# Small work moved, a halved load, a finer last pair and another order of the routing in a one-layer decoder kernel

## The reference

```python
h = rmsnorm(x, g_mix)
pa, pb, pc, pd = split(h @ w_in)            # w_in: 1024 x 2816
o_a = moba_attention(...)                   # four branches, 4 heads of 64 each
o_b = diff_attention(..., lam, ...)         # lam = exp(lq1.lk1) - exp(lq2.lk2) + 0.2
o_c = stick_breaking_attention(...)
o_d = sliding_window_attention(...)         # A, B, D add a relative position bias (table of 32 buckets)
merged = sum(sigmoid(h @ w_gate[i]) * (branches[i] @ w_br[i]) for i in range(4))
x = x + merged @ w_o                        # w_o: 1024 x 1024
x = x + hierarchical_moe(rmsnorm(x, g_ffn), ...)  # top group of 4, top 2 of its 8 experts
out = rmsnorm(x, g_final)
```

## Time and profile before

| | |
|---|---|
| device time, median of 3 runs (lowest to highest) | 717.75 us (717.66 to 717.78) |
| the profiled execution, its own time | 719.13 us |
| its span | 717.3 us |
| TensorE busy | 685.7 us, 96% |
| VectorE busy | 245.9 us, 34% |
| ScalarE busy | 192.0 us, 27% |
| GpSimd busy | 4.2 us, 1% |
| moved by DMA | 243.56 MB, mean 340 GB/s |

### The profile page before, as it was taken

How to read it: one execution, slowest core, us unless ns; L and a number is a source line. 1 busy time by engine, 2 the same in 40 slices (tenths; PEclk the granted TensorE clock), 3 DMA queues, 4 the chain that set the end, 5 groups by cost and what they waited for, 6 DMA issues and landing times.

```text
span 717.3 us, 9888 instructions
## 1 busy us (share of the span) xinstructions
PE 685.7 (96%) x4042; PEld 401.6 (56%) x4042; DVE 245.9 (34%) x526; ACT 192.0 (27%) x304; POOL 4.2 (1%) x8
## 2 busy tenths in 40 slices
PE   8999999999999999999999999999989899898995
PEld 6899887777777874344344344344334343442432
DVE  7463556766567673121121121122121020210212
ACT  5551565598563521100100100001000010000112
POOL 0000000000000000000000000000000000000000
PEclk9999999999999999999999999999999999998998
DMA  8899631374439978999999999999999999999992
GB/s 308 284 273 286 215 117 59 118 259 152 176 118 343 406 307 292 409 428 426 426 427 426 425 428 426 429 426 428 428 429 426 429 427 428 424 428 429 414 399 104
DMA packets 46125, 243.56 MB, mean 340 GB/s; under 512 B 10192, under 2 KB 13448, under 8 KB 33800
## 3 DMA queue, kind: packets, MB, share of 16 engines
q1 hardware_dynamic: 45640, 241.45, 84.6%
q0 software_dynamic: 448, 1.59, 0.7%
HBM read 241.96 MB, written 1.07 MB: 339 GB/s over the span
## 4 chain that ended last, share of the span: by engine, by line
PE 63%; DMA 22%; SPq 6%; DVE 5%; ACT 2%; issue 2%; POOLq 0%; DVEq 0%; ACTq 0%
PE bank L1713 21%; DMA unit<-in_w 20%; PE bank L1768 8%; PE bank L1386 7%; PE bank L1387 7%; PE bank L1388 7%; SPq L548 5%; PE bank L1691 4%; DMA unit<-in_w_in 2%; DVE low L332 2%; PE bank L1780 1%; PE bank L1781 1%; PE bank L1742 1%; PE bank L1478 1%; ACT high L327 1%
## 5 line engine op out<-in xcount | busy, mean ns | idle before, releaser
L1713 PE MATMUL bank<-unit,xT 128*64 128x512 f32 x1024 | 230.8, 604 | 14.0 <-DMA unit<-in_w 12.3
L1713 PEld LDWEIGHTS bank<-unit,xT 128*64 128x64 f32 x1024 | 76.0, 139 | 153.5 <-issue 147.1
L1768 PE MATMUL bank<-unit,hidT 128*64 128x512 f32 x480 | 106.3, 595 | 0.0
L1386 PE MATMUL bank<-high,hT_hi 128*128 128x512 f32 (+2 forms) x208 | 79.8, 384 | 2.4 <-DVE low L332 2.4
L1387 PE MATMUL bank<-low,hT_hi 128*128 128x512 f32 (+2 forms) x208 | 77.3, 372 | 0.0
L332 DVE TENSOR_TENSOR low<-unit,high 128x2048 fp32r<-128x2048 f32 (+1 forms) x34 | 70.7, 2099 | 11.4 <-ACT high L327 11.4
L1768 PEld LDWEIGHTS bank<-unit,hidT 128*64 128x64 f32 x480 | 33.1, 137 | 61.5 <-issue 60.0
L1388 PE MATMUL bank<-high,hT_lo 128*128 128x512 f32 (+2 forms) x176 | 65.1, 370 | 0.0
L327 ACT ACTIVATE high<-unit 128x2048 fp32r<-128x2048 f32 (+1 forms) x34 | 58.9, 1756 | 8.4 <-PE bank L1388 5.1
L1263 DVE TENSOR_TENSOR y_lo<-bank,y_hi 128x512 fp32r<-128x512 f32 x30 | 20.7, 691 | 94.1 <-ACT y_hi L793 94.1
L1691 PEld LDWEIGHTS bank<-pick,hk 128*128 128x128 bf16 x768 | 44.4, 98 | 13.5 <-issue 12.2
(11 more groups left out here) (252 smaller groups left out, 688.0 us busy)
## 6 DMA issues: line engine op xcount, KB each, us to landing
unit<-in_w SPq DMA_DIRECT2D x86, 2048.0 KB, 30.1
unit<-in_w_gate SPq DMA_DIRECT2D x8, 2048.0 KB, 9.9
unit<-in_w SPq DMA_DIRECT2D x12, 1024.0 KB, 26.6
unit<-in_w SPq DMA_DIRECT2D x14, 512.0 KB, 9.0
unit<-in_w_in SPq DMA_DIRECT2D x3, 2048.0 KB, 15.9
unit<-in_w_br SPq DMA_DIRECT2D x4, 1024.0 KB, 6.0
unit<-in_w_o SPq DMA_DIRECT2D x2, 2048.0 KB, 10.6
unit<-in_w_in SPq DMA_DIRECT2D x6, 512.0 KB, 7.6
```

The costliest lines, as they stand in the source:

```text
L1386: mm(dst, a_hi, b_hi, start=first, stop=False)
L1713: last = mm(bank[4 + w][g * CAP:(g + 1) * CAP, :], xT[:, k, g * CAP:(g + 1) * CAP], rhs, start=(k == 0), stop=(k == KD - 1))
L1768: last = mm(bank[6 + n][g * CAP:(g + 1) * CAP, :], hidT[:, c, g * CAP:(g + 1) * CAP], rhs[:, c, n * BANK:(n + 1) * BANK], start=(c == 0), ...
```

## The change

Nine edits, all in the order or grain of work; the arithmetic stays but for one subtraction.

1. Stage 1, loads: unit 1 comes in two loads of 1 MB with a semaphore each, and ScalarE's first high part of it waits for the first half alone.
2. Stage 1, small work: on VectorE `dvec` moves behind the copy of block 5, the other small operations behind the low parts of unit 4, the end of lam behind those of unit 5; the exponential on ScalarE moves behind the high parts of unit 5. 23 instead of 18 idle products at the very start.
3. Start of stage 2: of the three waits for banks read out, the one for bank 4 moves behind the first scores.
4. Step 7: a low part goes ahead of the sums of squares.
5. Stage 3: half of `branch(3, 3)` goes ahead of the first `turn_tile`.
6. Routing: x is turned by blocks of 128 neighbouring columns (`turn_rows`) with router weights loaded to match and a second copy of g_ffn (1024 elements of 4 bytes); three quarters of the turning stand ahead of the end of the last w_o product, and router products and absorptions behind it. 36 idle products for 20. `remain(3)` goes to GpSimd; on ScalarE the squares and norm of the last quarter go ahead of its first part. The slot numbers are raised by one once, so that the subtraction at line 1199 goes.
7. The last pair: 12 pieces for 9; `combine(p - 1, [0])` goes ahead of `up(1)`; hidden, its turning, and its copy go in two halves, the second in bank 5.
8. Stores: in the order in which the parts are ready.
9. The overflow branch, which is not run here, waits for matrices in pairs.

The core of the diff:

```diff
-LAST_PIECES = ((0, 0, 0, 0, 4), (0, 0, 0, 4, 8), (0, 2, 0, 0, 4), (0, 2, 0, 4, 6), (0, 2, 0, 6, 8),
-               (0, 4, 0, 0, 4), (0, 4, 1, 0, 2), (0, 4, 1, 2, 3), (0, 4, 1, 3, 4))
+LAST_PIECES = ((0, 0, 0, 0, 4), (0, 0, 0, 4, 8),
+               (0, 2, 0, 0, 2), (0, 2, 0, 2, 4), (0, 2, 0, 4, 6), (0, 2, 0, 6, 7), (0, 2, 0, 7, 8),
+               (0, 4, 0, 0, 2), (0, 4, 0, 2, 4), (0, 4, 1, 0, 2), (0, 4, 1, 2, 3), (0, 4, 1, 3, 4))
...
+                if u == 1:
+                    sp.dma_start(dst[:, 0:4, :], src[:, 0:4, :]).then_inc(s["second_half"], 16)
+                    dst, src = dst[:, 4:, :], src[:, 4:, :]
                 sp.dma_start(dst, src).then_inc(s_unit[u % RING1], 16)
...
-            for t in range(NT):
-                for n in range(2):
-                    sp.wait_ge(*((s[("half0", "half1")[t]], 1) if n == 0 else (s["scaled"], t + 1)))
-                    cols = slice(n * BANK, (n + 1) * BANK)
-                    sp.dma_start(out[0, t * P:(t + 1) * P, cols], xg[:, t, cols]).then_inc(s["stored"], 16)
+            for t, n, ready, count in ((0, 1, s["scaled"], 1), (1, 0, s["half1"], 1), (1, 1, s["scaled"], 2), (0, 0, s["half0"], 1)):
+                sp.wait_ge(ready, count)
+                cols = slice(n * BANK, (n + 1) * BANK)
+                sp.dma_start(out[0, t * P:(t + 1) * P, cols], xg[:, t, cols]).then_inc(s["stored"], 16)
...
+            t, cols, qs = quarter(3)
+            pool.wait_ge(s["parts1"], 4)
+            pool.wait_ge(s["parts3"], 2)
+            nc.gpsimd.tensor_tensor(remainder[1][:], x[:, t, cols].rearrange("p (q k) -> p k q", k=KD), hk_1[:, t, :, qs],
+                                    ALU.subtract).then_inc(s["remains"], 1)
...
-            act.wait_ge(s["lamx"], 1)
-            nc.scalar.activation(lam[:, 2:4], lam[:, 0:2], ACT.Exp).then_inc(s["lame"], 1)
             for u in range(6):
...
                 for half in range(2 if u < 5 else 0):
                     high_part(act, u + 2, half)
+                if u == 3:
+                    act.wait_ge(s["lamx"], 1)
+                    nc.scalar.activation(lam[:, 2:4], lam[:, 0:2], ACT.Exp).then_inc(s["lame"], 1)
...
                         nc.vector.tensor_scalar(dst, src, scale, None, ALU.mult).then_inc(s["projD"], 1)
+                    if i == 5:
+                        bias_vectors()
                 for half in range(2 if u < 5 else 0):
                     low_part(dve, nc.vector, u + 2, half)
+                if u == 2:
+                    constants()
+                elif u == 3:
+                    weight_of_difference()
...
+            branch(3, 3, [0])
             pe.wait_ge(s["mrg"], 14)
-            turn_tile(0, merged, s["mTps"])
-            branch(3, 3)
+            turn_tile(0)
+            branch(3, 3, [1])
...
+            for b in (0, 1):
+                read_out(b)
             scores_ahead(0)
+            read_out(4)
...
             first_part(2)
             second_part(2)
-            first_part(3)
             row_squares(3)
             second_norm(1)
+            first_part(3)
             second_part(3)
...
             weighted_turned(1, 1)
-            remain(3)
             second_norm(1)
...
-            link(V.tensor_scalar(slot[:], slot[:], -1.0, None, ALU.add))
...
+                for half, done in enumerate((s["last_half"], z["hid"])):
+
+                    of = lambda ap: ap.rearrange("p (q c) -> p q c", c=CE)[:, :, 2 * half:2 * half + 2]
+                    V.scalar_tensor_tensor(out=of(hid[:]), in0=of(sg[:]), scalar=slot_gate[:], in1=of(bank[5][:]),
+                                           op0=ALU.mult, op1=ALU.mult).then_inc(done, 1)
...
+                    combine(main, p - 1, [0])
                     up(1, main, p, slots, here)
-                    combine(main, p - 1, [0])
-                    turn_hidden(main, p)
+                    turn_half(main, p, 0)
                     combine(main, p - 1, [1])
+                    turn_half(main, p, 1)
```

More of the change, by code:

```diff
@@ L185, in hybrid_decoder_layer @@
         wo_lo = place("wo_lo", [P, KD, TOK], F32R, offset=shared)
+        h2T = [place(f"h2T{t}", [P, KD, TOK], offset=(hT_at, shared)[t]) for t in range(NT)]
         sig_at = at[0]
@@ L318, in high_part @@
                 act.wait_ge(first_pieces[piece], 16)
+            elif xi == 1 and piece == 0:
+                act.wait_ge(s["second_half"], 16)
             else:
@@ L782, in experts @@
                     link(nc.scalar.activation(warm, warm, ACT.Sqrt))
-                act.wait_ge(z["hTp"], p + 1)
                 if not first:
                     act.wait_ge(z["Y"], 2 * p)
-                nc.scalar.activation(hidT[:].rearrange("p c q -> p (c q)"), bank[4][:], ACT.Copy).then_inc(z["hT"], 1)
+                if last:
+                    for half, (ready, done) in enumerate(((s["last_half"], s["last_half"]), (z["hTp"], z["hT"]))):
+                        act.wait_ge(ready, 2 if half == 0 else p + 1)
+                        nc.scalar.activation(hidT[:, 2 * half:2 * half + 2, :].rearrange("p c q -> p (c q)"),
+                                             bank[4 + half][:, 0:TOK], ACT.Copy).then_inc(done, 1)
+                else:
+                    act.wait_ge(z["hTp"], p + 1)
+                    nc.scalar.activation(hidT[:].rearrange("p c q -> p (c q)"), bank[4][:], ACT.Copy).then_inc(z["hT"], 1)
                 if not first:
@@ L1132, in second_norm, with logits @@
                 V.reciprocal(rs[:, t:t + 1], rs[:, t:t + 1]).then_inc(s["rs"], 1)
+            def logits(t):
+                dve.wait_ge(s["lg_ps"], t + 1)
+                dve.wait_ge(s["rs"], t + 1)
+                return V.scalar_tensor_tensor(out=lg[:, t, :], in0=bank[4 + t][:, 0:NG + NE], scalar=rs[:, t:t + 1],
+                                              in1=rbias[:], op0=ALU.mult, op1=ALU.add)
             add_product(0, 0).then_inc(s["x1"], 1)
@@ L1160, in _ @@
             from_end = lambda n: cst[:, C_IOTA:C_IOTA + n].unsqueeze(1).broadcast_to([P, NT, n])
-            R = NG + NE
-            for t in range(NT):
-                dve.wait_ge(s["lg_ps"], t + 1)
-                dve.wait_ge(s["rs"], t + 1)
-                link(V.scalar_tensor_tensor(out=lg[:, t, :], in0=bank[4 + t][:, 0:R], scalar=rs[:, t:t + 1],
-                                            in1=rbias[:], op0=ALU.mult, op1=ALU.add))
             link(V.tensor_reduce(m[:, 0, :], lg[:, :, 0:NG], AX, ALU.max))
@@ L1245, in gathered, with hidden @@
                                     ALU.mult).then_inc(z["xT"], 1)
-            def hidden(z, p, first=False):
+            def hidden(z, p, first=False, last=False):
                 dve.wait_ge(z["sg"], p + 1)
@@ L1270, in experts @@
                     picks(main, p + 1, p + 1)
-                hidden(main, p, first)
+                hidden(main, p, first, last)
                 if not last:
@@ L1608, in _, with turn_tile, turn_rows @@
             branch(D_, 1, [0])
-            def turn_tile(t, rows, done):
+            def turn_tile(t):
                 for i in range(2):
                     for kk in range(4):
-                        k_th = rows[:, t, :].rearrange("p (q k) -> p k q", k=KD)[:, 4 * i + kk, :]
+                        k_th = merged[:, t, :].rearrange("p (q k) -> p k q", k=KD)[:, 4 * i + kk, :]
                         last = nc.tensor.transpose(bank[2 * t + i][:, kk * P:(kk + 1) * P], k_th, ident)
-                    last.then_inc(done, 1)
+                    last.then_inc(s["mTps"], 1)
+            def turn_rows(t, i):
+                pe.wait_ge(s["x1"], TURNED[t, i])
+                for k in range(4 * i, 4 * i + 4):
+                    last = nc.tensor.transpose(bank[2 * t + i][:, (k % 4) * P:(k % 4 + 1) * P], x[:, t, k * P:(k + 1) * P], ident)
+                last.then_inc(s["h2ps"], 1)
             def out_product(t, n, ks=range(KD)):
@@ L1724, in turn_hidden, with turn_half @@
                 last.then_inc(z["hTp"], 1)
+            def turn_half(z, p, half):
+                pe.wait_ge(*((z["hid"], p + 1) if half else (s["last_half"], 1)))
+                for c in range(2):
+                    c_th = hid[:].rearrange("p (q c) -> p c q", c=CE)[:, 2 * half + c, :]
+                    last = nc.tensor.transpose(bank[4 + half][:, c * P:(c + 1) * P], c_th, ident)
+                last.then_inc(z["hTp"] if half else s["last_half"], 1)
             def turn_picks(z, p):
```

114 lines of the change are left out of this document (63 added, 51 removed).

## The result

The changed kernel takes 720.34 us (median of 20 runs, 718.22 to 726.15) against 717.82 for the kernel before (20 runs, 717.42 to 720.18): a ratio of 1.0037, 95% interval 1.0026 to 1.0048, so 2.5 us slower. The forecast was 720.7. The profiled execution has a span of 719.3 us against 717.3. The stream of expert weights is full to the end as before and starts later.

The account below looks back on a forecast made before the run. It took the DMA stream of expert weights as the bound, shifted by TensorE's first up product; +2.9 + 2.3 - 0.7 + 0 - 0.3 - 0.45 - 0.8 = +2.95 us on the 717.75 median gave 720.7, range 716.6 to 723.4.

Parts of the forecast that it names:

- the wait released by `dvec`: Sign in stage 1: TensorE idle about 5 us before block 7, until VectorE's dvec, directly behind unit 2's low parts.
- the half clock behind it: Sign in stage 1: a granted clock of 0.5 in the windows from 38 to 41 us.
- the missing idle rows before unit 1's halves: Sign in stage 1: TensorE no longer has idle rows before the two halves of unit 1.
- Stage 1, +5.2 less 0.7: Up to the scores: waiting for dvec +2.9 us, clock loss +2.3; moved wait for bank 4 at the scores -0.7.
- Step 7, 0: Low part ahead of the sums of squares: ScalarE's root still runs at 151.4, so 0 us (-0.3 to +0.3).
- branch(3, 3) in halves, -0.3: Stage 3: TensorE's 0.80 us idle before 227.69 is filled; out_product starts at 229.8 instead of 230.06, -0.3 us.
- Routing, -0.45: Before the experts: new order of turnings and router products 0.2 us earlier, slot subtraction gone -0.25; -0.45 (-1.0 to +0.2).
- The term for the subtraction: Routing: the subtraction of slots, 0.19 us at 264.62, goes with the gap behind it, -0.25 us.
- GpSimd's subtraction: Routing rival: remain(3) on GpSimd blocks VectorE's chain over the shared SBUF interface, 1.6 to 3.2 us more; chance 0.10.
- The end, -0.8: Last pair and stores: finer pieces and new order -0.3 us, stores issued as ready -0.5; -0.8 (-2.4 to 0).
- A fixed time after the first up product: Expert stage: the weight stream ends a fixed time after that product, so each microsecond there is one of the whole.
- unit 2 early, and all edits earn: Stage 1 rival: unit 2 lands at 26 instead of 30.2, no clock fall, -3.55 us, 714.2; chance 0.15.

Follow-up runs that it names:

- e6: The kernel before with only VectorE's small work and lam's exponential moved as in the change, dvec behind unit 2's low parts: 720.42 us, ratio 1.0034.
- e1: The changed kernel with dvec made ahead of unit 2's low parts: 713.52 us, ratio 0.9941 to the kernel before.
- e4: The changed kernel with 18 idle products on TensorE in the wait for dvec: 720.91 us, ratio 1.0044 to the kernel before.
- e2: The changed kernel with step 7 as before, sums of squares ahead of the low part: 718.38 us, ratio 1.0013 to the kernel before.
- e8: e3 with remain(3) taken back from GpSimd to VectorE: 713.35 us, ratio 0.9938 to the kernel before.
- e3: The changed kernel with dvec ahead of unit 2's low parts and step 7 as before: 713.47 us, ratio 0.9937 to the kernel before.
- e9: e3 with the four stores issued in the order of before: 715.57 us, ratio 0.9968 to the kernel before.
- e5: The kernel before with only unit 1 loaded in two halves: 716.60 us, ratio 0.9980.
- e10: e3 with the last pair as before (nine pieces, hidden rows in one product, combine behind up): 714.11 us, ratio 0.9951 to the kernel before.
- e7: The kernel before with only the small work and lam's exponential moved, but dvec ahead of unit 2's low parts: 716.74 us, ratio 0.9983.

## Why the prediction was right, and where it was not

Direction, size and the deciding mechanism were right: `dvec` behind the low parts makes TensorE wait at block 7, the clock falls behind it, and the later start of the experts carries it to the end. e6 shows that the moved small work alone makes the loss, and e1 that putting `dvec` back ahead of the low parts turns the whole change into a gain of 4.3 us. But the sum was right by luck, because two terms were wrong in opposite ways: up to the first up product it had +3.75 and the traces show +3.73, of which the scores have 2.25 instead of 4.5 and step 7 has 1.9 instead of 0. On the profiled executions the whole sum, +2.95, was too large: their spans differ by 2.0. Of the signs named ahead, the wait released by `dvec`, the half clock behind it and the missing idle rows before unit 1's halves are there; the low parts of unit 2 started at 31.00, a little ahead of the forecast 32.

- **Stage 1, +5.2 less 0.7: mis-sized.** Measured +2.25 at the scores. Unit 2 landed at 29.05, not 30.2, so block 7 started at 36.33 instead of 37.6 and waited 4.42 instead of 5.4: its load was issued 0.5 earlier than before and took 15.2 us instead of 15.9. The clock missed 1.71 us of full speed and cost 1.3 at the scores, by e4, not 2.3. These two, 1.3 and 1.0, are the 2.25 by which the term was too large. In the traces of e2 and e6 the landing is at 30.30 and 30.09, the clock misses 3.41 us of full speed, and the scores are 4.25 and 5.04 late (e6 has the 0.56 ahead of the scores still): the 4.5 of the forecast is inside what single executions show. I took the spread of one load for a constant.
- **Step 7, 0: the step that failed.** The prediction said that the root could not run before 151.4 "the same", because it added the low part's 2.28 and the sums' 1.4 to 147.7. It left out that the low part must wait for ScalarE's high part: here 0.45 us before 150.48, with the stage 2.25 late. The root came 2.70 late, not 2.25, and TensorE lost as much to the chain behind it as it gained by the vanished 0.78, and 0.4 more. Against the changed kernel e2 measured 2.0 us; the waits are 0.4 of that, the rest appears with a fall of the clock that two other traces of the same order don't have.
- **branch(3, 3) in halves, -0.3:** -0.2 measured (4.15 to 3.95).
- **Routing, -0.45:** -0.22. The term for the subtraction held (-0.25 against -0.23), that for the order did not: behind the last w_o product it takes 4.2 us instead of 4.7 as forecast 4.1, but that product now ends 0.5 later by the turnings inside it (258.69 against 254.23, from a start 3.95 late), and the two cancel.
- **GpSimd's subtraction.** Rows: it ran from 261.77 to 263.17, and VectorE's logits at 263.00 and its chain at 263.29 and 263.48 kept their pace, 0.16 and 0.17 an instruction. e8 finds no difference in time. The rule of the Trainium skill ("SBUF — State Buffer", "Who interferes with whom") is neither borne out nor refuted by this: the instruction at 263.00 reads PSUM for one input, and the first with two SBUF inputs, at 263.48, comes after GpSimd's end.
- **The end, -0.8: too small.** Last pair and stores gave -1.4 in the traces. From the wait near 650 to the last combine it is 54.85 us with the new last pair and 55.45 with the old: -0.6, where I had -0.3; the wait of 0.64 for the half of the hidden rows was right, but so was the piece for which nobody waits now. The stores gave -0.8 instead of -0.5: counted from GpSimd's start the last is issued 0.59 us earlier (2.37 behind it instead of 2.96) and lands in 2.5 us instead of 2.7. Two of the four are issued before GpSimd is done at 715.58, as forecast.
- **"A fixed time after the first up product": nearly.** From the first up product to the last combine all kernels need 438.8 to 440.6 us. The changed kernel's start is 3.73 late and its last combine 2.78; 0.6 of the difference is the last pair, the other 0.35 has no row.

The rival "unit 2 early, and all edits earn" put 714.2 on a load that came at 26. Such a time was reached, 713.5, but by `dvec`'s place and not by the load.

The best versions measured are e1, e3 and e8 (713.52, 713.47, 713.35), which the runs can't tell apart: 4.3 us below the kernel before.

## What to carry to other kernels

When small work is moved behind large work "because it is needed later", list every product of it and find its first reader: here five of six results could wait, and the sixth, 0.55 us long, had a reader at once. An in-order engine that is waiting for a load is the place for such an instruction, ahead of the work that waits. And a forecast whose sum fits should still be checked term by term, since two of mine cancelled.

## What the runs showed of the hardware

- The granted clock falls by the piece. Summed over windows of 1 us, each fall before 700 us in the traces of these kernels cost 1.7 us of full speed, or twice that: e6 shows 3.41 behind a wait of 4.48, the changed kernel 1.71 behind 4.42, and e3 nothing behind waits of 2.10 and 2.20, but 1.71 behind one of 2.19.
- It can fall with TensorE busy in every window. In e1, e8 and e9 it fell at 254 to 256 us, in the router's products of 36 columns and the absorptions behind them; in e1 no idle row of TensorE stands between 228 us and the fall, though busy time of TensorE is modelled. Two of its windows:

```profile
254.00:255.00 1.00, 1.00 (x11) 0.92 (x9) 0.86 (x3) 0.71 (x1) 0.21 (x1) 1.00 1.00 401
...
256.00:257.00 1.00, 1.00 (x3) 0.64 (x3) 0.47 (x3) 0.76 (x2) 0.19 (x1) 0.50 1.03 434
```

- The landing of one load, that of unit 2, issued at 13.4 to 14.3 us, varied from 27.6 (e5) to 30.4 us (e10) between traces, and the runs of the kernels in which `dvec` waits behind it spread further (718.2 to 726.2 over 20 runs, 718.8 to 723.5 for e6) than those of the others on the same base (717.4 to 720.2 before, 716.0 to 717.3 for e5, 715.8 to 717.5 for e7).
- 18 matmuls added in stage 1 or in the expert stage went with a 28th packet of 16 KB on the instruction queue, which came among the stores, and with an end 1.5 to 2.2 us longer, in three kernels of three; the eleven kernels with 27 such packets had neither. That the one makes the other isn't shown.
